# Expert stage of a diffusion block: eight row buffers for U and four for V, in place of four and eight

## The reference, cut to what matters

```
idx  = the 16 best experts of 128 x 128, from two score tables      # route
gate = softmax(score)
u    = w_u[idx]                                                    # 16 gathered rows for each token
act  = gelu(sum_d u[k, d] * h[d])                                  # 16 dot products
out += sum_k gate[k] * act[k] * w_v[idx[k]]                        # 16 gathered rows again
```

## Time and profile before

| | before |
|---|---|
| device time, median of 3 runs | 3575.17 us |
| the runs | 3572.12 to 3575.26 us |
| span of the profiled execution, first to last instruction | 3572.6 us |
| expert stage, first gather to last instruction | 2144.9 to 3572.6 us |
| busy over the span: PE, DVE, ACT, POOL | 80%, 64%, 27%, 49% |
| gathers (queue of POOL): packets, volume | 73728, 536.90 MB |

### The profile page before, as it was taken

How to read it: one execution, slowest core, us unless ns; L and a number is a source line. 1 busy time by engine, 2 the same in 40 slices (tenths; PEclk the granted TensorE clock), 3 DMA queues, 4 the chain that set the end, 5 groups by cost and what they waited for, 6 DMA issues and landing times.

```text
span 3572.6 us, 43685 instructions
## 1 busy us (share of the span) xinstructions
PE 2841.5 (80%) x15344; PEld 2093.1 (59%) x15344; DVE 2281.9 (64%) x2628; ACT 960.9 (27%) x1306; POOL 1740.4 (49%) x948
## 2 busy tenths in 40 slices
PE   8878677598988889999988882877776778686677
PEld 3557566498966689999988871434342434242233
DVE  2377777788065588999989347555555555555542
ACT  1255354343145444333333320111111111011100
POOL 0133424277433267778767626544444444444442
PEclk9988888799989999999989995999998999899999
DMA  7522212365222256565556549999998999899997
GB/s 300 207 88 70 88 65 84 116 227 220 100 89 71 78 216 246 215 233 219 220 220 234 206 147 378 411 381 411 386 415 350 417 393 393 356 389 391 385 422 301
DMA packets 126150, 905.57 MB, mean 253 GB/s; under 512 B 14000, under 2 KB 15216, under 8 KB 16368
## 3 DMA queue, kind: packets, MB, share of 16 engines
q0 software_dynamic: 73728, 536.90, 36.6%
q1 hardware_dynamic: 38304, 278.94, 21.7%
q10 hardware_dynamic: 14032, 88.72, 6.3%
HBM read 900.28 MB, written 4.23 MB: 253 GB/s over the span
## 4 chain that ended last, share of the span: by engine, by line
PE 31%; DVE 30%; DMA 20%; issue 11%; ACT 4%; POOL 2%; DVEq 1%; ACTq 0%; POOLq 0%
PE ps L413 13%; DVE macc L1189 12%; DMA u<-in_peer_u,idx 11%; DMA v<-in_peer_v,idx 7%; PE ps L687 6%; PE ps L442 3%; PE ps L662 2%; DVE u L1428 2%; DVE aa L1146 1%; POOL u L1496 1%; PE ps L471 1%; PE ps L427 1%; PE ps L429 1%; PE ps L428 1%; PE ps L588 1%
## 5 line engine op out<-in xcount | busy, mean ns | idle before, releaser
L1482 POOL TENSOR_TENSOR wl<-w,wh 128x1024 fp32r<-128x1024 f32 x432 | 1102.3, 2563 | 983.0 <-ACT wh L732 982.1
L687 PE MATMUL ps<-v,dg 128*128 128x512 f32 x2048 | 945.9, 616 | 314.6 <-ACT dg L1016 164.3
L1428 DVE SCALAR_TENSOR_TENSOR u<-u,hN 128x2048 f32<-128x2048 f32 x256 | 583.2, 2291 | 496.5 <-DMA u<-in_peer_u,idx 496.3
L687 PEld LDWEIGHTS ps<-v,dg 128*128 128x128 f32 x2048 | 390.6, 196 | 865.5 <-issue 698.0
L413 PE MATMUL ps<-hx_hi,wh 128*128 128x256 f32 x2368 | 700.8, 296 | 2.9 <-DVE y L1206 1.7
L732 ACT ACTIVATE wh<-w 128x1024 fp32r<-128x1024 f32 x432 | 453.8, 1057 | 854.5 <-PE ps L413 578.7
L413 PE MATMUL ps<-hx_lo,wh 128*128 128x256 f32 x2368 | 681.5, 288 | 0.0
L413 PE MATMUL ps<-hx_hi,wl 128*128 128x256 f32 x2368 | 680.7, 287 | 0.0
L1189 DVE SCALAR_TENSOR_TENSOR macc<-mr,sT,macc 128x256 f32<-128x256 f32 x480 | 652.1, 1358 | 27.0 <-DMA mr<-in_wmod 10.2
L1496 POOL DMA_INDIRECT u<-in_peer_u,idx x256 | 329.5, 1287 | 696.3 <-DVE u L1428 535.9
L413 PEld LDWEIGHTS ps<-hx_hi,wh 128*128 128x128 f32 x2368 | 468.0, 198 | 11.4 <-issue 9.2
(11 more groups left out here) (231 smaller groups left out, 3231.8 us busy)
## 6 DMA issues: line engine op xcount, KB each, us to landing
w<-in_stream SPq DMA_DIRECT2D x264, 1024.0 KB, 4.8
mr<-in_wmod ACTq DMA_DIRECT2D x64, 1024.0 KB, 5.6
wg<-in_gates ACTq DMA_DIRECT2D x8, 512.0 KB, 3.4
u<-in_peer_u,idx POOLq DMA_INDIRECT x256, 16.4
v<-in_peer_v,idx POOLq DMA_INDIRECT x256, 17.7
xs<-in_ctx ACTq DMA_DIRECT2D x1, 2048.0 KB, 17.4
xs<-in_x ACTq DMA_DIRECT2D x1, 2048.0 KB, 23.7
x<-in_x ACTq DMA_DIRECT2D x1, 2048.0 KB, 7.5
```

What stands on the lines that cost most here:

```text
L687: last = mm(ps[:, b, :], dg[:, k % 4, :], V[n % NV][:, b * 512:(b + 1) * 512], start=(k == 0), stop=(k == TOPK - 1))
L1428: stt(U[n % NU][:, :], U[n % NU][:, :], 1.0, hN[:, t, :], ALU.mult, ALU.mult, accum_out=dot[:, t, k:k + 1])\
L1482: sub = lambda out_, a, b: nc.gpsimd.tensor_tensor(out_, a, b, ALU.subtract)
```

## The change

The number of buffers is exchanged: NU goes from 4 to 8, NV from 8 to 4. The four additional U buffers take the memory of the four V buffers that are gone. `acc` stays at its address. In the first pass the wait for `x2_stored` now stands ahead of U block 4, and the first four V blocks are issued after U block 7, no longer after U block 3. All semaphore waits that count by NU and NV follow.

```diff
-        NU, NV = 4, 8
-        U = [sb(f"u{i}", R_HC + 16384 + 8192 * i, [P, D]) for i in range(NU)]
-        V = [sb(f"v{i}", at, [P, D]) for i, at in enumerate(
-            [R_SPLIT + 8192 * i for i in range(4)] + [R_HX, R_HX + 8192, R_Y + 8192, R_Y + 16384])]
-        acc = sb("acc", R_HC + 16384 + 8192 * NU, [P, 2, D])
+        NU, NV = 8, 4
+        U = [sb(f"u{i}", at, [P, D]) for i, at in enumerate(
+            [R_HC + 16384 + 8192 * i for i in range(4)] + [R_HX, R_HX + 8192, R_Y + 8192, R_Y + 16384])]
+        V = [sb(f"v{i}", R_SPLIT + 8192 * i, [P, D]) for i in range(NV)]
+        acc = sb("acc", R_HC + 16384 + 8192 * 4, [P, 2, D])
...
             for k in range(TOPK):
+                if k == NV:
+                    pool.wait_ge(x2_stored, 32)
                 rows_u(0, 0, 0, k)
                 if k == NU - 1:
-                    pool.wait_ge(x2_stored, 32)
                     for kv in range(4):
                         rows_v(0, 0, 0, kv)
```

## The result

The changed kernel takes 3641.6 us, median of 4 runs (3641.2 to 3642.0), the one before 3573.6 in the same comparison (3571.7 to 3575.3). The ratio is 1.0189, interval 1.0175 to 1.0204: slower by 68 us, where 52 was forecast (the range ended at 3665). A second comparison gave 1.0188 (1.0174 to 1.0203). The profiled execution took 3641.96 us, its span is 3639.9.

What follows compares the result with a forecast made beforehand. The DMA's gather rate bounds the kernel, with about 96 us lost in pauses. Terms of -4, +32, +9 and +15 sum to +52 on the profiled 3572.6, and 2.6 more gives 3627 us; range 3595 to 3665.

Steps and rivals of the forecast that it cites:

- The place: POOL's standstill moves to V block 4, awaiting PE's block 0, 27.2 us after L (last V block landed) in pass 9.
- What is left after the release: From V block 4's release to the next L, 23 blocks left: 62.8 us, bounds 61.7 and 64.0.
- Passes without PE work ahead: Passes 2, 4, 6, 8, 10, 12, 13: release 2.8 us later, gain 3.4; cost -0.6 each, -4 in all.
- Odd passes: Passes 1, 3, 5, 7 cost 8.1 us each, +32; passes 9, 11 4.6 each, +9, including 2 for later keys.
- Pass 0: V block 4, free before, waits for PE: +18 us, less 3 for early U blocks; +15 booked (13 to 18).
- The last pass: Pass 15: PE's four-block round of 13.8 us hides 6.7 us landing plus some 2 for signal and issue; costs nothing.
- The argument for one more gather out: U block 4 also goes out before POOL stands: queue dry at L + 22.4 us, L + 19.9 before.
- U buffers were missing: Rival: more U blocks out close the DMA pauses; 3527 us if half close, 3560 if some; chance 0.07.
- Balance: Rival: one more block out and better refilling gain 6 to 7 us each pass; 3575 within 7 us; chance 0.06.
- starvation: Rival: four V buffers starve PE in the steady part too; 3654 us, or 3708 at the median's excess; chance 0.15.
- The price of a restart: After a pause the first V gather lands in 6.7 us; the skill's 4.4 would make the sum +20.
- Odd and even refills: By the skill's lock, late releases after the dot-product burst refill odd passes without loss: estimated 6 us less, 1 in each of six.

Runs made afterwards that it cites:

- diagonals first, four and eight: Kernel before (four U, eight V buffers) with ACT making diagonals 0 to 3 of each pass ahead of the next route's softmax: 3573.9 us, ratio 1.0000.
- keys early: The change (eight U, four V buffers) with the DMA of the keys issued at the start of a head's turn on ACT: 3597.8 us, ratio 1.0068.
- four and four: The change with the four additional U buffers taken away, so four U and four V buffers: 3635.1 us, ratio 1.0172.
- diagonals first: The change (eight U, four V buffers) with ACT making diagonals 0 to 3 ahead of the next route's softmax: 3570.6 us, ratio 0.9991.
- spread eight and four: The change with diagonals first, keys early, and PE's queries and scores put behind blocks 4, 8 and 12 in odd passes: 3511.5 us, ratio 0.9826.

## Why the prediction was right, point by point

- **The place.** Right. POOL stands at V block 4 for PE's block 0 of the same pass, and the end of that block could be read from diagonal 4 in the trace of before: 27.2 us after L in pass 9 before, 30.2 with the change; in the seven passes without PE work 25.4 as a mean, against 25.5.
- **What is left after the release.** Taken as 62.8 us; measured, from the end of PE's block 0 to the next L, 63.0 as the mean of 13 passes (61.8 to 63.9). The bounds held. Its parts were off and nearly cancel, which is luck: POOL follows block 0's end after 0.8 us (0.3 taken), and V block 4 lands 5.4 to 5.8 us after its issue in the odd passes and 5.9 to 7.4 us in the seven others (6.7 taken).
- **Passes without PE work ahead.** -4 forecast, +1.7 measured. Each is off by 0.8 us, the second largest share of what the sum missed: 63.3 us after the release in these and not 62.8, and 66.0 and not 66.2 before.
- **Odd passes.** Forecast 8.1 and 4.6 each; measured 8.4 to 10.1, and 6.1 and 5.9. The term for the keys was too small: one block more is out ahead of them, and they land 1.6 and 2.8 us later in passes 9 and 11 (I had 2), and 1.8, 1.3 and 2.2 us later in passes 3, 5 and 7 (I had none). Block 0 ended 3.0 and 3.4 us later in passes 9 and 11 and 2.4 in pass 7. In passes 3 and 5 it ended only 0.3 and 0.0 us later, as block 0 itself took 4.1 and 4.4 us in place of 5.7: that those two came near the forecast is luck. The kernel with four U buffers, whose keys land as before (25.2 to 25.8 us after L in passes 3, 5 and 7), shows that the block more is the cause.
- **Pass 0.** +15 forecast with a range of 13 to 18. The last dot product of pass 1 ends 19.2 us later (the instruction behind it starts at 2298.94, before at 2279.76), of which 1 us is a later start: the full +18, with nothing back from the early U blocks. The product of pass 0's block 0 ended at 2224.24 here and at 2223.89 before, although the dot products of pass 0 were done 1 us sooner (2204.8, 2205.9), since block 0 took 6.6 us and not 5.1. Passes 0 and 1 together came out near the 23 us forecast by luck: pass 1 gained 5.0 us after its release (67.5 us before, 62.5 after) where 3.4 had been taken.
- **The last pass.** Hidden as forecast: PE works 56.87 us without a pause, 55.19 before. The 1.7 us more are not the buffers: they are all in block 0, 5.37 us at a granted clock of 0.68 here and 3.67 us at 1.00 before, each behind a short pause of PE, and the other 15 blocks take 3.6 us each in both. The same 5.37 us occur with eight V buffers (diagonals first, four and eight), and 3.67 with four (keys early). The windows of block 0, after and before:

```profile
3571.70:3577.10 5.40, 5.38 (x9) 2.41 (x10) 0.00 (x0) 0.00 (x0) 0.00 (x0) 0.68 1.00 419
3506.20:3509.90 3.70, 3.70 (x9) 1.76 (x10) 0.00 (x0) 0.02 (x1) 0.00 (x0) 1.00 1.01 423
```

- **The argument for one more gather out** gave the right count of 23 blocks left and was wrong as a credit to the U buffers, as four and four showed: that gather finds its place in the pause even with four.
- **The rivals.** That U buffers were missing was true only once V's wait was out of the way, with the diagonals first: the condition named for it, a block 0 that ends within 15.4 us of L, is met there in the seven passes without PE work (9.8 to 11.5 us) and their pause closed. Balance and starvation did not come: the windows at 422 GB/s with four V buffers exclude the second.
- **The price of a restart.** No V gather of the changed kernel landed sooner than 5.4 us after its issue; 6.7 us was too long for the odd passes. By the fit of the Trainium skill (DMA: Bandwidth & Descriptors, Anatomy of one DMA), an estimated 4.4 us, the sum would have been +20. The trace does not agree with it.
- **Odd and even refills.** In the kernel before, 122 of the 124 gathers issued while a dot product ran took over 1.2 us to issue, and only 2 of the 388 others. In the change it is 62 of 190, and 1 of 322, so an issue beside a dot product is not always longer. From the release to L the odd passes took 62.7 us on average (1, 3, 5, 7, 9 and 11) and the seven others 63.3. By the lock of the Trainium skill (SBUF — State Buffer, SBUF: two separate sides) the odd passes would refill with less loss than the even ones. The trace agrees in direction, with 0.6 of the 1 us estimated from it; the passes of one group lie up to 1.7 us apart, and the landing of V block 4 alone differs by 1.0 (5.6 and 6.6 us on average), so that the loss after it is no smaller in the odd passes. No run changes this alone, so that a lock is the cause is not shown.

The sum was 15 us short of the +67.3: 6 in the passes without PE work, 6 in the odd passes from 3 on, 1 in passes 0 and 1, and the rest at the start and the end. The mechanism is the one forecast; of its largest term, the late block 0 of the odd passes, the later keys were counted in two passes of five.

What stays open: whether eight U buffers are 6 us slower than four in the order of the kernel, or the same; and why a pass with the same order has its block 0 done now in 3.7 and now in 5.4 us or more, which moves single passes by 1 to 2 us.

## What to carry to other kernels

Where one engine issues two streams in a fixed alternation, the stream with the later release stops both: find for each the instruction that frees its buffer, and compare the two moments with the moment at which the queue runs dry. In these kernels more buffers paid for the stream that was released last; the four additional U buffers were worth 0 or 90 us, depending on the order of two other engines. Long waits in the list are no evidence by themselves: waits of 535 us cost little when the queue holds out, and a wait for a small load of keys, 5 to 10 us in five passes and 16 in pass 1, cost 44.

## What the runs showed of the hardware

The gathers run at 422 GB/s with four or eight buffers for either stream, as long as their queue does not run dry (windows of 64 to 85 us in the kernel before, in diagonals first and in the spread eight and four). After a pause the first gather of 1 MB lands 5.4 to 7.4 us after its issue (V block 4 of passes 1 to 13 of the change). A DMA of 128 KB issued beside the gathers takes 7 to 10 us to land (keys at 2869.33, landed 2878.99, with two weight loads beside it), 2.4 to 5.1 us where no weights are loaded and the gathers are about to run dry (passes 9 and 11, before and after), and 2.2 us when little else moves (issued 2103.05, landed 2105.24 in the changed kernel): it is the small transfer behind the large ones that an engine waits for. In these traces the granted clock of PE was below 1.00 in a block done behind a pause of some microseconds (0.55 in block 0 of passes 2 before and 8 after, 0.63 and 0.68 above), and the eight instructions of a block then took 4.1 to 6.7 us in place of 3.6; it was not so behind every such pause (3.67 us at 1.00 in pass 15 before).
